# Token-major residual and norms, 512-column down and out projections, and a four-slot weight ring in a two-model transformer kernel

## The reference, cut to what matters

```python
def rmsnorm_2(x, g):
    y = xf * lax.rsqrt(jnp.mean(xf * xf, axis=-1, keepdims=True) + EPS)
def sublayer(x, shift, scale, gate, g_pre, g_post, fn, res_weight):
    h = rmsnorm_2(x, g_pre) * (1 + scale[:, None, :]) + shift[:, None, :]
    return x + res_weight * gate[:, None, :] * rmsnorm_2(fn(h), g_post)
def swiglu(h, w_gu, w_down):
    gate, up = jnp.split(h @ w_gu, 2, axis=-1)
    return (jax.nn.silu(gate) * up) @ w_down
```

## Time and profile before

| what | value |
|---|---|
| timed runs, median (lowest, highest) | 1570.95 us (1564.87, 1577.61) |
| span of the profiled execution | 1557.6 us |
| TensorE busy / VectorE / ACT / GpSimd | 93% / 69% / 46% / 7% of the span |
| granted TensorE clock, mean | 0.978 |
| DMA traffic | 337.58 MB, 217 GB/s over the span |
| one boundary between a feed-forward block and the next block | 14.6 us |

### The profile page before, as it was taken

How to read it: one execution, slowest core, us unless ns; L and a number is a source line. 1 busy time by engine, 2 the same in 40 slices (tenths; PEclk the granted TensorE clock), 3 DMA queues, 4 the chain that set the end, 5 groups by cost and what they waited for, 6 DMA issues and landing times.

```text
span 1557.6 us, 28387 instructions
## 1 busy us (share of the span) xinstructions
PE 1455.5 (93%) x10962; PEld 1397.8 (90%) x10962; DVE 1073.6 (69%) x1458; ACT 716.2 (46%) x934; POOL 102.7 (7%) x198
## 2 busy tenths in 40 slices
PE   6899989999989999999989999899999977899997
PEld 4888878999989999988889999799999876799996
DVE  5786695887767777678667886667786764555542
ACT  6514435555355443455455443454435543554432
POOL 0011000000100110100001110001100000000000
PEclk9999998999999999999999999999999989999998
DMA  8577232777866888856437887758976430255550
GB/s 346 228 252 248 95 109 71 266 257 243 291 235 210 320 292 296 300 184 220 150 112 280 304 317 279 250 178 308 335 274 241 149 135 28 84 213 173 182 187 27
DMA packets 60726, 337.58 MB, mean 217 GB/s; under 512 B 6880, under 2 KB 7264, under 8 KB 32112
## 3 DMA queue, kind: packets, MB, share of 16 engines
q1 hardware_dynamic: 32544, 234.67, 41.7%
q0 software_dynamic: 27936, 101.72, 19.2%
q10 hardware_dynamic: 176, 0.16, 0.0%
HBM read 335.49 MB, written 1.05 MB: 216 GB/s over the span
## 4 chain that ended last, share of the span: by engine, by line
PE 78%; DVE 10%; DMA 4%; ACT 4%; issue 2%; DVEq 0%; POOLq 0%; POOL 0%; SPq 0%; ACTq 0%
PE bank L194 22%; PE bank L195 22%; PE bank L196 22%; PE bank L199 12%; DMA mring<-m_stream 4%; DVE wlo L188 3%; DVE mring L351 1%; ACT whi L182 1%; DVE T L324 1%; DMA raw<-w_stream 1%; DVE hlo L329 1%; ACT lnt L287 0%; ACT SQ L272 0%; DVE T L399 0%; DVE mx L1734 0%
## 5 line engine op out<-in xcount | busy, mean ns | idle before, releaser
L194 PE MATMUL bank<-hhi,whi 128*128 128x256 f32 x2280 | 651.7, 286 | 26.4 <-DVE hlo L329 19.4
L195 PE MATMUL bank<-hlo,whi 128*128 128x256 f32 x2280 | 646.7, 284 | 0.0
L196 PE MATMUL bank<-hhi,wlo 128*128 128x256 f32 x2280 | 646.5, 284 | 0.0
L188 DVE TENSOR_TENSOR wlo<-raw,whi 128x2048 fp32r<-128x2048 f32 x219 | 500.6, 2288 | 159.2 <-ACT whi L182 155.9
L182 ACT ACTIVATE whi<-raw 128x2048 fp32r<-128x2048 f32 x219 | 417.6, 1909 | 259.3 <-PE bank L196 222.8
L194 PEld LDWEIGHTS bank<-hhi,whi 128*128 128x128 f32 x2280 | 438.9, 192 | 32.8 <-issue 24.0
L195 PEld LDWEIGHTS bank<-hlo,whi 128*128 128x128 f32 x2280 | 439.3, 193 | 0.3
L196 PEld LDWEIGHTS bank<-hhi,wlo 128*128 128x128 f32 x2280 | 439.1, 193 | 0.0
L351 DVE SCALAR_TENSOR_TENSOR mring<-mring,cb 128x1024 f32<-128x1024 f32 x192 | 233.7, 1221 | 133.3 <-DMA mring<-m_stream 133.0
L195 PE MATMUL bank<-hid_lo,whi 128*128 (+1 forms) x880 | 249.0, 283 | 0.0
L196 PE MATMUL bank<-hid_hi,wlo 128*128 (+1 forms) x880 | 248.6, 282 | 0.0
(11 more groups left out here) (233 smaller groups left out, 1142.1 us busy)
## 6 DMA issues: line engine op xcount, KB each, us to landing
raw<-w_stream SPq DMA_DIRECT2D x219, 1024.0 KB, 6.4
mring<-m_stream POOLq DMA_DIRECT2D x192, 512.0 KB, 5.1
con<-const_d SPq DMA_DIRECT2D x1, 1472.0 KB, 10.4
X<-xT SPq DMA_DIRECT2D x1, 1024.0 KB, 11.4
XC<-ctxT SPq DMA_DIRECT2D x1, 1024.0 KB, 9.4
cb<-c_row POOLq DMA_DIRECT2D x2, 512.0 KB, 5.3
y<-X SPq DMA_DIRECT2D x1, 1024.0 KB, 3.9
cols<-cols_d SPq DMA_DIRECT2D x1, 222.5 KB, 7.4
```

Of the source, the lines that this page charges most:

```text
L188: nc.vector.tensor_tensor(wlo[:, c % 3], raw[:, c % 3], whi[:, c % 3].bitcast(f32), ALU.subtract).then_inc(s_lo, 1)
L194: nc.tensor.matmul(out, wh, rhi, start=start, stop=True, skip_group_check=True)
L195: nc.tensor.matmul(out, wh, rlo, start=False, stop=True, skip_group_check=True)
L196: return nc.tensor.matmul(out, wl, rhi, start=False, stop=True, skip_group_check=True)
```

## The change

Residual and norms: `X` becomes [128 tokens, 2, 1024]. Squares are summed along the row by ACT itself (`act_row_rstd`), so the statistics matmuls go. The post norm's gain and gate become a row (`crow`), stored to DRAM and loaded back spread over partitions (`act_gate_row`); VectorE multiplies a bank by it (`dve_product`) and adds (`dve_update`), 512 columns at a time. The normalised input is turned back to features by TensorE, 8 fp32 matmuls against a diagonal of reciprocal roots per token tile (`pe_pre`), then scaled, rounded and split (`dve_pre_split`, `act_pre`). x is transposed once at the start; the key/value input is made at the boundary f2 to f3 from the same turned tiles.

Down and out chunks: 128 tokens stationary, 512 weight columns moving, bank 2t+h for token tile t and half h. The last two down chunks (the last out chunk) are taken bank by bank (`pe_out_last`), so that bank 0 is complete first; in feed-forward blocks `pe_pre` of token tile 0 stands ahead of the fourth bank.

Ring: four slots; `wlo` lies on `raw`, so the split is in place and SP loads chunk c once TensorE has used chunk c-4. Up projections use four banks in turn. All loops are unrolled. The first modulation's columns come straight out of TensorE, with weight tiles stationary. The output is stored in four parts.

```diff
-        raw = sb("raw", [P, 3, CW])
-        whi = sb("whi", [P, 3, CW], f32r)
-        wlo = sb("wlo", [P, 3, CW], f32r)
+        raw = sb("raw", [P, SLOTS, CW])
+        raw_at = nc.sbuf_base - SLOTS * CW * 4
+        wlo = nc.alloc_sbuf_tensor_at("wlo", [P, SLOTS, CW], f32r, offset=raw_at)
+        whi = sb("whi", [P, SLOTS, CW], f32r)
+        X = sb("X", [P, 2, D])
+        crow = sb("crow", [P, D])
+        junk = sb("junk", [P, 512])
+        dg = sb("dg", [P, 2, P])
+        ss = sb("ss", [P, len(ROW_NORMS), 2])
...
-        def act_split(act, c, i=None):
+        def act_split(act, c):
-            act.wait_ge(s_raw[c % 3], 16 * (c // 3 + 1) + run(i, 16))
-            if c >= 3:
-                act.wait_ge(s_pe, c - 2 + run(i, 3))
-            nc.scalar.activation(whi[:, c % 3], raw[:, c % 3], ACT.Copy).then_inc(s_hi, 1)
-        def dve_split(dve, c, i=None):
+            act.wait_ge(s_raw[c % SLOTS], 16 * (c // SLOTS + 1))
+            if c >= SLOTS:
+                act.wait_ge(s_pe, c - SLOTS + 1)
+            nc.scalar.activation(whi[:, c % SLOTS], raw[:, c % SLOTS], ACT.Copy).then_inc(s_hi, 1)
+        def dve_split(dve, c):
...
+        def mm3w(out, c, w, hi, lo, start):
+            wh, wl = whi[:, c % SLOTS, w:w + 512], wlo[:, c % SLOTS, w:w + 512]
+            mm(out, hi, wh, start)
+            mm(out, hi, wl, False)
+            return mm(out, lo, wh, False)
...
-        def pe_down_chunk(pe, c, khi, klo, first, last=False):
-            order = [(g, m + n) for m in range(0, DT, 2) for g in range(2) for n in range(2)] if last else \
-                [(g, m) for g in range(2) for m in range(DT)]
-            for g, m in order:
-                ins = mm3(down(m), c, g * DT + m, khi[g], klo[g], first and g == 0 and m % 2 == 0)
-                if last and g and m % 2 and m < DT - 1:
-                    ins.then_inc(s_down, 1)
+        GROUPS = [(t, h) for t in range(2) for h in range(2)]
+        def pe_out_chunk(pe, c, k0, hi, lo, first):
+            for g in range(2):
+                for t, h in GROUPS:
+                    ins = mm3w(out_bank(t, h), c, g * D + h * 512, tok(hi, k0 + g, t), tok(lo, k0 + g, t),
+                               first and g == 0)
             ins.then_inc(s_pe, 1)
...
+        def pe_out_last(pe, chunks, k0, hi, lo, mid=None):
+            for i, (t, h) in enumerate(GROUPS):
+                if i == 3 and mid is not None:
+                    mid()
+                for n, c in enumerate(chunks):
+                    for g in range(2):
+                        k = k0 + 2 * n + g
+                        ins = mm3w(out_bank(t, h), c, g * D + h * 512, tok(hi, k, t), tok(lo, k, t), False)
+                    if i == 3:
+                        ins.then_inc(s_pe, 1)
+                if i < 3:
+                    ins.then_inc(s_yb, 1)
...
+        def pe_pre(pe, pre, t):
+            if pre is None:
+                return pe_final(pe, t)
+            pe.wait_ge(s_dg, 2 * PRES.index(pre) + t + 1)
+            for b in range(2):
+                for jj in range(4):
+                    j = 4 * b + jj
+                    ins = mm(turned(t, b)[:, jj * P:(jj + 1) * P], X[:, t, j * P:(j + 1) * P], dg[:, t], True)
+                ins.then_inc(s_tpn, 1)
...
+        def act_row_rstd(act, n, src, wait, out=False, between=None):
+            for h in range(2):
+                act.wait_ge(*wait(h))
+                ins = nc.scalar.activation(junk[:], src(h), ACT.Square, accum_out=ss[:, n, h:h + 1])
+                if out:
+                    ysq[0] += 1
+                    ins.then_inc(s_ysq, 1)
+                    act.wait_ge(s_ysq, ysq[0])
+                else:
+                    alink(act, ins)
+                if h == 0:
+                    alink(act, nc.scalar.activation(uu[:, n:n + 1], ss[:, n, 0:1], ACT.Identity, bias=eps[:, 0:1],
+                                                    scale=1.0 / D))
+                    if between is not None:
+                        between()
+            alink(act, nc.scalar.activation(rl[:, n:n + 1], ss[:, n, 1:2], ACT.Ln, bias=uu[:, n:n + 1], scale=1.0 / D))
+            nc.scalar.activation(rr[:, n:n + 1], rl[:, n:n + 1], ACT.Exp, scale=-0.5).then_inc(s_rr, 1)
...
+        def act_boundary(act, stage):
+            pre = NEXT[stage]
+            act.preload_act_table_set(LN_EXP)
+            for t in range(2):
+                if stage not in PLAIN:
+                    act_row_rstd(act, rn("post", stage, t), lambda h: out_bank(t, h),
+                                 lambda h: out_ready(stage, t, h), True,
+                                 (lambda: act_pre(act, pre, 0)) if t and pre else None)
+                x0 = XU[stage] + (4 if stage == "f0" else 2) * t
+                if stage == "f0":
+                    act_row_rstd(act, rn("fin", stage, t), lambda h: xrow(t, h), lambda h: (s_xu, x0 + h + 1))
+                    x0 += 2
+                if pre:
+                    act_row_rstd(act, rn("pre", pre, t), lambda h: xrow(t, h), lambda h: (s_xu, x0 + h + 1))
+                    if t or stage in PLAIN:
+                        act_pre(act, pre, t)
...
+        def dve_pre(dve, pre, t):
+            p = PRES.index(pre)
+            n = rn("pre", pre, t)
+            dve.wait_ge(s_rr, n + 1)
+            nc.vector.tensor_scalar(dg[:, t], ident, rr[:, n:n + 1], None, ALU.mult).then_inc(s_dg, 1)
...
+        def dve_product(dve, stage, t, h):
+            si = STAGES.index(stage)
+            if h == 0 and t == 0:
+                dve.wait_ge(s_crow, 16 * (si + 1))
+            if stage in PLAIN:
+                dve.wait_ge(*out_ready(stage, t, h))
+            else:
+                dve.wait_ge(s_ysq, 4 * POSTS.index(stage) + 2 * t + h + 1)
+            if t:
+                dve.wait_ge(s_xu, XU[stage] + h + 1)
+            twc[0] += 1
+            nc.vector.tensor_tensor(TW[:, h], out_bank(t, h), crow[:, h * 512:(h + 1) * 512],
+                                    ALU.mult).then_inc(s_tw, 1)
+        def dve_update(dve, stage, t):
+            x0 = XU[stage] + (4 if stage == "f0" else 2) * t
+            for h in range(2):
+                dve.wait_ge(s_tw, twc[0] - 1 + h)
+                if stage in PLAIN:
+                    nc.vector.tensor_tensor(xrow(t, h), xrow(t, h), TW[:, h], ALU.add).then_inc(s_xu, 1)
+                else:
+                    n = rn("post", stage, t)
+                    dve.wait_ge(s_rr, n + 1)
+                    nc.vector.scalar_tensor_tensor(out=xrow(t, h), in0=TW[:, h], scalar=rr[:, n:n + 1],
+                                                   in1=xrow(t, h), op0=ALU.mult, op1=ALU.add).then_inc(s_xu, 1)
...
+        def dve_boundary(dve, stage):
+            pre = NEXT[stage]
+            for t in range(2):
+                dve_product(dve, stage, t, 0)
+                if t and pre:
+                    dve_pre_split(dve, pre, 0)
+                dve_product(dve, stage, t, 1)
+                dve_update(dve, stage, t)
+                if pre:
+                    dve_pre(dve, pre, t)
+                else:
+                    dve.wait_ge(s_tpn, 4 * len(PRES) + 2 * t + 1)
+                    nc.vector.tensor_copy(OUT[:, 0:4, t * P:(t + 1) * P], four(turned(t, 0)[:])).then_inc(s_fo, 1)
+            if pre:
+                dve_pre_split(dve, pre, 1)
...
+        def act_gate_row(act, stage, part):
+            si = STAGES.index(stage)
+            src = mod[:, 16:24] if stage == "lstm" else mod[:, 40:48] if stage == "f0" else coef[:, POST_COEF[stage]]
+            if part == 0:
+                act.wait_ge(s_cgo, si + 1)
+                act.dma_start(rows_d[si].rearrange("(j p) -> p j", p=P), src,
+                              allow_slow_non_contiguous=True).then_inc(s_cgd, 16)
+            else:
+                act.wait_ge(s_cgd, 16 * (si + 1))
+                act.dma_start(crow[:], rows_d[si].partition_broadcast(P)).then_inc(s_crow, 16)
...
+            last = FT // 2 - 2
+            for d in range(last):
+                pe.wait_ge(s_lo, c0 + FT + d + 1)
+                pe.wait_ge(s_hid, FT * f + 2 * d + 2)
+                pe_out_chunk(pe, c0 + FT + d, 2 * d, hid_hi, hid_lo, d == 0)
+            pe.wait_ge(s_lo, c0 + FT + last + 2)
+            pe.wait_ge(s_hid, FT * (f + 1))
+            pre = NEXT[f"f{f}"]
+            pe_out_last(pe, (c0 + FT + last, c0 + FT + last + 1), 2 * last, hid_hi, hid_lo,
+                        lambda: pe_pre(pe, pre, 0))
...
+        DOWN_UNITS = [0, 0] + [1, 1, 2] * 3
...
             def chunks(a, b):
                 for c in range(a, b):
-                    sp.wait_ge(s_lo, c - 2)
-                    sp.dma_start(raw[:, c % 3], w_stream[c]).then_inc(s_raw[c % 3], 16)
+                    if c >= SLOTS:
+                        sp.wait_ge(s_pe, c - SLOTS + 1)
+                    sp.dma_start(raw[:, c % SLOTS], w_stream[c]).then_inc(s_raw[c % SLOTS], 16)
...
             for k in range(DT):
-                pe.wait_ge(s_lo, k + 1)
```

(8 more changed lines are left out.)

732 lines of the change are left out of this document (399 added, 333 removed).

## The result

The changed kernel takes 1640.83 us (median of four runs, 1633.83 to 1644.27) against 1567.91 us before (four runs). The ratio is 1.046, 95% interval 1.040 to 1.052. The forecast was 1588 with a range to 1611. The direction was right; the size, 73 us instead of 17, was not.

A forecast was written before the change was run, and what follows sets the result against it. TensorE, busy 1455.5 of 1557.6 us, was taken as the bound, with seams waiting. Terms -13.3 + 21.6 + 2 - 6 - 3 + 16.8 - 1 = +17.1 gave span 1574.7; 13.4 above it, 1588 us, range 1552 to 1611.

The forecast's parts named there:

- The start: First modulation: columns come without copy and transposes, but the weights behind wait for TensorE; -1 us, between -4 and +3.
- the seam walk: Between blocks: step-by-step timing of TensorE, ACT and VectorE; six seams +21.6 us, f3 +2, end -6, overlap allowance -3.
- Gate rows: Two DMAs a stage on ACT's queue, waited for a dozen chunks later: nothing, at most 2 us.
- Rival (c): Mid-stream: late loads after seams and modulation units starve the ring, 0.25 us for 132 chunks, +33 us, 1621; chance 0.08.
- In mid-stream this hides, and I cost it at nothing: Four-slot ring: load, copy and split take 10.6 us against three chunks' 16.5 us, so later requests cost nothing.
- The 512-column projections: Down and out chunks: 0.229 us a matmul, 0.26 us less a chunk, 51 chunks, -13.3 us (0 to -16).
- Rival (d): Down and out projections: no effective widening, as 128-column weights of hid load slower than hhi's; +30 us, 1601; chance 0.05.
- The clock: Seams: long idle stretches restart TensorE at the lower clock, fourteen at 1.2 us, +16.8 us (0 to +32).
- The sum: Whole kernel: all terms together +17.1 us on the span, 1574.7, which makes 1588 as the median; chance 0.45.
- (a): Seams wait as walked, but the clock stays up because turning counts as work: 0 us, 1571; chance 0.27.
- (b): Seams: load of chunk e+1 and modulation units aren't on the path, clock half as costly; -12 to -15 us, 1556; chance 0.15.

The follow-up runs named there:

- the base: Changed kernel with the first modulation as before and feed-forward gate and gain rows stored by partition, put in tile order by ACT; 1592.14 us, ratio 1.0167.
- the run by partition: Changed kernel with gate and gain rows stored in (partition, tile) order, 32 bytes a partition, VectorE reading them back strided; ratio 1.0415.
- the fillers: Unread matmuls on constants ahead of token tiles' turnings: added to the changed kernel, 1.0409; to the base with chunk e+1's copy and split behind tile 0's norm, 1.0067.

## Why the prediction was right, and where it failed

**"The start: ... I take -1, between -4 and +3".** This step failed, by 26 us. It named what the change removes (a copy and transposes) and what the weights behind wait for, but never multiplied 256 new products by a duration, and never asked at which clock they would run. The rows had the duration: the earlier trace rows shows six passes of 128 columns in 0.83 us, which the seam walk itself reads as 0.22 for two. At 0.11 us each, 256 are 28 us; with two trains of statistics (3.6 each) and the turning of x (1.9), behind the first chunk at 8.4, they would end at 46, where the old start ends. This is an estimate, and by it a term near nothing could stand. At the lower clock they are 54 us, and that is what came: 213 ns each for 34 us and again from 53.8 on. The trace of before shows the lower level at its start as well. Its first 14 products of 512 columns come 0.43 us apart, the next ones 0.23:

```profile
15.87 0.63 PE L199 MATMUL bank<-wlo,c 128*128 128x512 f32 x1
16.30 0.63 PE L199 MATMUL bank<-whi,c 128*128 128x512 f32 x1
...
18.77 0.40 PE L199 MATMUL bank<-wlo,c 128*128 128x512 f32 x1
19.00 0.40 PE L199 MATMUL bank<-whi,c 128*128 128x512 f32 x1
```

**"Gate rows: two DMAs a stage ... nothing, at most 2".** This failed by 15 to 23 us: 0.0096, or 15 us, between the run with the old modulation alone and the base; 22.5 us in the up windows between the changed kernel and the run by partition; 23 us added to the kernel before. The step counted bytes, 4 KB a store. It noted the rule of the Trainium skill ("DMA: Bandwidth & Descriptors", Rules for kernel authors) that a store whose last dimension is strided makes a descriptor for each element, found no row with such a store, and dropped it. "No row" was a reason to bound the cost from above, not for nothing. The trace agrees with the rule: packets under 512 B rose from 6880 (the line below, before) to 16432, and nine stores of 1024 are 9216 of these 9552.

```profile
DMA packets 60726, 337.58 MB, mean 217 GB/s; under 512 B 6880, under 2 KB 7264, under 8 KB 32112
```

**Rival (c), the ring starves in mid-stream: 1621, chance 0.08.** It had the right symptom, waits for chunk splits in the up projections, and nearly the right amount, 27 of its 33 us. Its mechanism was wrong for nearly all of it: not the two late loads after a seam, but the store, 22.5 us. "In mid-stream this hides, and I cost it at nothing" was right of the ring but for the 3 us in f3 that stay without the store.

**The seam walk.** Right in its mechanism, some 8 us short in all (+26.6 for +18, with wide chunks and clock). f1's first wait: 10.92 for 9.9; mLSTM to f0: +8.4 where walk, wide chunks and clock make +10; the end: -7.3 for -8; f2: +3.6 for +3. Too small for f0 (+10.9 for +6) and f1 (+6.5 for +3). f0's trace has 2.1 us of waits for chunks inside the down projection too. What stands ahead of tile 0 was named rightly: taking the chunk and the units away cut the wait from 8.62 to 2.24. Between the tiles the walk was short: first matmul at 35.0 after e-3's end, where it had 29.8. Of these 5.2 us, 1.1 come from the longer load and 3.1 from turning and group four at the lower clock (3.8 and 3.9 for 1.8 and 2.75), which the sum held in its clock term; the last 1 us is tile 1's turning, at the lower clock too (3.6).

**The 512-column projections.** Right: 252 in 57.85 us, 0.229 each, in f1, f2, f3 and f4. Rival (d) is out.

**The clock, +16.8.** Every seam has its stretches at half, as forecast; the mean went from 0.978 to 0.953. As a cost it measured some 17 us, once the 8.7 that the fillers lose at the end are put aside: the size was right, though known to some 11 us only.

**The sum.** With the two failed terms taken out of the kernel (but for three stores), the base measures 1.0167, +26 us, interval +16 to +36. The forecast's +17 lies inside. Rivals (a) at 1571 and (b) at 1556 are out for this base as well.

No kernel here beats the one before: the closest, at 1.0067 (1.0041 to 1.0093), is still slower. What is left in its profile is mLSTM's stage with its seam (222.2 us against 213.5), f0's down projection with its seam (82.5 against 77.9), f3's up projection (131.8 against 128.5) and the 4.6 us of fillers at the end. From tile 0's turning to tile 1's are 14.9 us in f0's seam, 12.9 in those of f1, f2 and f3, and 9.3 in the other three; making that chain shorter wasn't tried.

## What to carry to other kernels

Price an edit by the number of instructions and of DMA pieces it adds, each times the nearest row of a trace at the clock level of that place, before asking what hides it; the two edits that looked like tidying (a copy saved, 4 KB stored) cost two thirds of the loss. A transposed store goes in an order that keeps each partition's run whole, with the reordering done by an idle engine; putting it where no load is in flight wasn't tried. An experiment's own cost has to be read from its trace, stage by stage, before its total is taken for the term: the fillers hid half of the clock's. Where a chunk is asked for at the end of its slot's use, look at what stands in the in-order lists behind its copy: the last one before a seam belongs behind the seam's first work, but only where that engine isn't the next to be waited for.

## What the runs showed of the hardware

- A store of 1024 elements of 4 bytes holds back the loads beside it: in the changed kernel 23 of those issued from 2 us before such a store to 15 us after it took 10 to 17 us. In f1's up projection 1 MB took 13.3 us (median of three) in place of 5 to 6, with traffic down to 17 GB/s. Six such stores cost 23 us in the otherwise unchanged kernel. The same 4 KB in 32-byte runs left no load over 10 us behind the start.
- 160 products in a row of 4, or of 128, moving columns, each with a new weight tile, went at 213 ns from 8.4 to 42.8 us. Behind 16 statistics matmuls of 256 columns they went at 112; then the four-column ones fell back as the record shows a granted clock of 0.5 from 53.8, the 128-column ones didn't. The record of the clock begins at 47 us in these two traces, and at 17.1 us in the one of before, just where the pitch of its first products falls from 0.43 to 0.23 us. So the 1.00 or 0.90 that windows give for the start says nothing of the part ahead.
- A VectorE product of 512 columns whose second input is read at a stride of 32 bytes took 1.11 us instead of 0.69. ACT's copy at the same stride took 1.24 us.
- Executions of one kernel differ with the clock granted: 19 runs of the kernel before lay between 1552.5 us (0.985) and 1581.1 us (0.973). A single profiled execution can thus be 10 us or more off its kernel's median.
